# Two chunked scans: log decays by a mask matmul, or by cumulative sums broadcast from DRAM

## The reference

```
a_cs  = cumsum(adt)                       # over the 128 steps of a chunk
decay = exp(a_cs[l] - a_cs[s])  for s <= l, else 0
y_diag = (c . b) * decay @ (x * dt)
```

## Time and profile before

| | |
|---|---|
| time, three runs | median 1102.46 us (1102.23 to 1104.29) |
| profiled execution, first to last instruction | 1102.2 us |
| TensorE busy | 1065.5 us, 97% |
| VectorE busy | 662.8 us, 60% |
| ScalarE busy | 442.9 us, 40% |
| GpSimd busy | 215.7 us, 20% |
| DMA | 123.89 MB, 112 GB/s over the span |
| granted TensorE clock, mean | 0.988 |

### The profile page before, as it was taken

How to read it: one execution, slowest core, us unless ns; L and a number is a source line. 1 busy time by engine, 2 the same in 40 slices (tenths; PEclk the granted TensorE clock), 3 DMA queues, 4 the chain that set the end, 5 groups by cost and what they waited for, 6 DMA issues and landing times. The chain is left out here.

```text
span 1102.2 us, 14509 instructions
## 1 busy us (share of the span) xinstructions
PE 1065.5 (97%) x5590; PEld 876.1 (79%) x5590; DVE 662.8 (60%) x1139; ACT 442.9 (40%) x826; POOL 215.7 (20%) x161
## 2 busy tenths in 40 slices
PE   9999999999989999999899999999999988989997
PEld 5888888888778877788778788887888866878886
DVE  4246435741056687766736866666595667966635
ACT  4223224332256562231623334348624448225432
POOL 0000000000000052201300100002104754135792
PEclk9999999999989999999999999999999999999999
DMA  8276634322042050232324345435212231203501
GB/s 301 81 271 215 215 102 145 114 80 95 11 136 56 10 197 5 73 134 77 125 77 153 115 153 191 153 115 172 91 63 77 63 111 58 77 20 103 185 1 77
DMA packets 58306, 123.89 MB, mean 112 GB/s; under 512 B 5760, under 2 KB 6016, under 8 KB 58112
## 3 DMA queue, kind: packets, MB, share of 16 engines
q1 hardware_dynamic: 55792, 110.22, 29.9%
q0 software_dynamic: 2304, 12.58, 3.2%
q10 hardware_dynamic: 144, 0.20, 0.0%
HBM read 108.83 MB, written 14.16 MB: 112 GB/s over the span
## 5 line engine op out<-in xcount | busy, mean ns | idle before, releaser
L287 DVE TENSOR_TENSOR w_lo<-raw,w_hi 128x2048 fp32r<-128x2048 f32 x58 | 134.3, 2315 | 207.9 <-ACT w_hi L283 196.9
L283 ACT ACTIVATE w_hi<-raw 128x2048 fp32r<-128x2048 f32 x51 | 97.6, 1913 | 211.4 <-PE projections_ps L131 138.3
L129 PE MATMUL projections_ps<-projections_x_hi,w_hi 128*128 128x512 f32 x208 | 81.1, 390 | 0.4 <-ACTq L506 0.4
L130 PE MATMUL projections_ps<-projections_x_lo,w_hi 128*128 128x512 f32 x208 | 80.9, 389 | 0.0
L131 PE MATMUL projections_ps<-projections_x_hi,w_lo 128*128 128x512 f32 x208 | 80.9, 389 | 0.0
L129 PE MATMUL projections_ps<-w_hi,projections_x_hi 128*128 128x512 f32 x192 | 74.7, 389 | 0.0
L130 PE MATMUL projections_ps<-w_lo,projections_x_hi 128*128 128x512 f32 x192 | 74.7, 389 | 0.0
L131 PE MATMUL projections_ps<-w_hi,projections_x_lo 128*128 128x512 f32 x192 | 74.7, 389 | 0.0
L244 DVE SCALAR_TENSOR_TENSOR resid<-resid,mixer_cw 128x512 f32<-128x512 f32 x96 | 64.9, 745 | 0.0
L2480 POOL TENSOR_TENSOR mixer_es<-masks,mixer_gsel 128x1024 f32<-128x1024 f32 x8 | 17.3, 2165 | 229.5 <-PE mixer_ps L1902 152.2
L129 PE MATMUL output_ps<-w_hi,output_m_hi 128*128 128x512 f32 x128 | 52.9, 413 | 2.5 <-DVE output_m_lo L1267 1.4
(11 more groups left out here) (330 smaller groups left out, 2583.3 us busy)
## 6 DMA issues: line engine op xcount, KB each, us to landing
raw<-in_w_in SPq DMA_DIRECT2D x26, 1024.0 KB, 5.0
raw<-in_gdn_w_in SPq DMA_DIRECT2D x24, 1024.0 KB, 5.0
tok<-in_ada_w POOLq DMA_DIRECT2D x16, 768.0 KB, 6.3
raw<-in_w_out SPq DMA_DIRECT2D x8, 1024.0 KB, 5.0
qkv_kept<-mixer_ring SPq DMA_DIRECT2D x8, 1024.0 KB, 4.2
mixer_st<-qkv_kept SPq DMA_DIRECT2D x32, 256.0 KB, 2.9
raw<-in_gdn_w_out SPq DMA_DIRECT2D x8, 1024.0 KB, 5.1
resid<-in_att_bias SPq DMA_DIRECT2D x16, 256.0 KB, 2.7
```

Of the source, the lines that this page charges most:

```text
L129: nc.tensor.matmul(out, w_hi, x_hi, start=first, stop=False, skip_group_check=True)
L130: nc.tensor.matmul(out, w_hi, x_lo, start=False, stop=False, skip_group_check=True)
L283: self.nc.scalar.activation(self.hi[s][:], self.raw[s][:], ACT.Copy).then_inc(self.hi_ready, 1)
L287: engine.tensor_tensor(self.lo[s][:], self.raw[s][:], self.hi[s][:], ALU.subtract)\
```

## The change

The decay matrix is now exp(-relu(c_l - c_s)), s in the partitions,, from cumulative sums c = -cumsum(log decay).

1. Two small float32 matmuls with `upper` make all cumulative sums of a layer, once with rows of heads and chunks (`logs_t`) and once with the 128 steps in the partitions (`logs`); ScalarE copies both out, negated. In layer one this stands at the start of attention; in layer two ahead of convolution block 4 (`LOGS_AT`), and the last column tile of that block's first half waits until the bank is read.
2. SP writes `logs_t` to DRAM, and later loads one row of 1024 values for each step, broadcast to the 128 partitions (512 KB), into `steps_in` or `steps`. The place of each load in SP's list is in the diff.
3. GpSimd subtracts the column of the partition's own step in place, for all 8 matrices in one instruction.
4. ScalarE clips with Relu in place, then takes Exp with scale -1.
5. The `below` matmuls, their PSUM banks and the waits on `seg_made` go; so do `gsel` and its copy on VectorE. GpSimd starts its list in the second mixer with a wait for `logs_out` and clears a stage's semaphores there.

```diff
 # scan stage, SP
+            def load_logs(s):
+                g = s % G
+                if s >= G:
+                    sp.wait_ge(e_ok, s - 1)
+                sp.dma_start(steps_in[:, g].rearrange("p h l -> p (h l)"), a["logs"][s].partition_broadcast(P))\
+                    .then_inc(logs_in[g], 16)
+            sp.wait_ge(logs_kept, 16)
+            for s in range(G):
+                load_logs(s)
             sp.dma_start(resid[:], a["x"].rearrange("(t p) d -> p t d", p=P)).then_inc(rows_in, 16)
...
-            for u in range(2, 6):
+            for u in range(2, 4):
                 load_unit(u)
+            for s in range(G, STEPS - 1):
+                load_logs(s)
+            for u in range(4, 6):
+                load_unit(u)
+            load_logs(STEPS - 1)
 # scan stage, PE (ahead_of)
-                pe.wait_ge(steps_ok, s + 1)
-                if s:
-                    pe.wait_ge(e_ok, s)
-                for n in range(2):
-                    mm = nc.tensor.matmul(ps[:, SEG + n, :], below, steps_in[:, g, 4 * n:4 * n + 4, :]...)
-                mm.then_inc(seg_made, 1)
 # scan stage, ACT (ahead_of)
-                act.wait_ge(seg_made, s + 1)
+                act.wait_ge(steps_ok, s + 1)
                 if s >= G:
                     act.wait_ge(yd_made, s - 1)
-                nc.scalar.activation(E[:, g], ps_seg, ACT.Exp).then_inc(e_ok, 1)
+                nc.scalar.activation(steps_in[:, g], steps_in[:, g], ACT.Relu).then_inc(clipped, 1)
+                act.wait_ge(clipped, s + 1)
+                nc.scalar.activation(E[:, g], steps_in[:, g], ACT.Exp, scale=-1.0).then_inc(e_ok, 1)
 # scan stage, GpSimd
             def scan_steps(s):
-                if s >= G:
-                    pool.wait_ge(seg_made, s - 1)
-                nc.gpsimd.tensor_tensor(steps_in[:, g], upper..., adt[:, c, heads_of(g)]..., ALU.mult)
+                pool.wait_ge(logs_in[g], 16 * (s // G + 1))
+                here = logs[:, c, heads_of(g)].unsqueeze(2).broadcast_to([P, HPG, P])
+                nc.gpsimd.tensor_tensor(steps_in[:, g], steps_in[:, g], here, ALU.subtract).then_inc(steps_ok, 1)
 # second mixer, SP
+            def load_logs(i, j):
+                if j:
+                    sp.wait_ge(e_ok, at(i, 1, j - 1, 1))
+                elif i:
+                    sp.wait_ge(z_ok, 8 * (HB - 1))
+                else:
+                    sp.wait_ge(logs_kept, 16 * TT)
+                sp.dma_start(flat(steps), a["logs2"][i * HB + j].partition_broadcast(P)).then_inc(logs_in, 16)
...
             stage(0, 2)
+            load_logs(0, 1)
             load(B_CONV + 2)
             sp.wait_ge(kk_made, at(0, 1, 1, 1))
             stage(0, 3)
+            load_logs(0, 2)
             sp.wait_ge(kk_made, at(0, 1, 2, 1))
             stage(0, 0)
+            load_logs(0, 3)
             load(B_CONV + 3)
...
             stage(1, 0)
+            load_logs(1, 0)
...
             sp.wait_ge(kk_made, at(1, 1, 0, 1))
             stage(1, 2)
+            load_logs(1, 1)
             sp.wait_ge(kk_made, at(1, 1, 1, 1))
             stage(1, 3)
+            load_logs(1, 2)
             sp.wait_ge(kk_made, at(1, 1, 2, 1))
             stage(1, 0)
+            load_logs(1, 3)
 # second mixer, ACT
             def exps(i, j):
-                act.wait_ge(seg_made, at(i, 1, j, 1))
+                act.wait_ge(steps_ok, at(i, 1, j, 1))
...
-                nc.scalar.activation(E, psZ[:]..., ACT.Exp).then_inc(e_ok, 1)
+                nc.scalar.activation(steps, steps, ACT.Relu).then_inc(clipped, 1)
+                act.wait_ge(clipped, at(i, 1, j, 1))
+                nc.scalar.activation(E, steps, ACT.Exp, scale=-1.0).then_inc(e_ok, 1)
```

More of the change, by code:

```diff
@@ L298, in channels @@
             for e in range(4):
+                if s == 0 and e == 3 and before_last:
+                    before_last()
                 for kk in range(HALF):
@@ L665, in _, with attention @@
                     w.tokens(pe, i * 2 + (N_Z + j), (N_Z + j) % 2, ps, x_hi, x_lo, banks_free)
-def attention(nc, a, ahead, mix_in, raw, m_g, resid, masks, qk, vals, tok, bias_in):
+def attention(nc, a, ahead, mix_in, raw, m_g, resid, masks, qk, vals, tok, bias_in, adt, logs, logs_t, logs_kept):
     ctx = Phase(nc, "attention")
@@ L767, in values @@
                     pe.wait_ge(y_done, 4 * (h - 1))
+                if n == 0 and h == 1:
+                    pe.wait_ge(logs_out, 2)
                 for qt in PARTS[n]:
@@ L776, in _ @@
             scores(0)
+            nc.tensor.matmul(ps_o[0:LOGS, 1, 0:P], flat_adt, masks[:, UPPER, :], start=True, stop=True)
+            nc.tensor.matmul(ps_o[:, 1, P:P + LOGS], masks[:, UPPER, :], flat_adt, start=True, stop=True).then_inc(logs_made, 1)
             for h in range(ATT_HEADS):
@@ L868, in _, with scan_and_output @@
                     exponentials(a_next, TILES[3:])
-def scan_and_output(nc, a, ahead, wba, wba_in, mix_in, split, raw, att_f, m_g, masks, small, resid, row_f, tok, xbc, dt, adt, modc,
-                    g_col, gain):
+def scan_and_output(nc, a, ahead, wba, wba_in, mix_in, split, raw, att_f, m_g, masks, small, resid, row_f, tok, xbc, dt, adt, logs,
+                    logs_kept, modc, g_col, gain):
     w_v = a["w_out"][0].rearrange("(k p) c -> p k c", p=P)
@@ L925, in scan_and_output @@
         turned, m_hi_ok, m_lo_ok = sem("turned"), sem("m_hi_ok"), sem("m_lo_ok")
-        steps_ok, seg_made, e_ok = sem("steps_ok"), sem("seg_made"), sem("e_ok")
+        steps_ok, clipped, e_ok = sem("steps_ok"), sem("clipped"), sem("e_ok")
+        logs_in = [sem(f"logs_in{i}") for i in range(G)]
         xs_turned, xs_out, x_read, xskip_ok = sem("xs_turned"), sem("xs_out"), sem("x_read"), sem("xskip_ok")
@@ L1433, in second_mixer @@
     NB, HB = 2, 4
+    ended = Phase.take_used()
     ctx = Phase(nc, "mixer2")
@@ L1688, in _ @@
                 if n == 6:
+                    sp.wait_ge(logs_out, 2)
+                    rows_out = a["logs2"].rearrange("r (x c l) -> c (r x) l", c=TT, l=P)
+                    for c in range(TT):
+                        sp.dma_start(rows_out[c], logs_t[V_HEADS * c:V_HEADS * (c + 1), :]).then_inc(logs_kept, 16)
                     sp.wait_ge(spilled[0], 32)
@@ L1692, in _ @@
                         stage(0, j)
+                    load_logs(0, 0)
             load(B_CONV + 1)
@@ L1821, in _, with logs_read @@
             tr.then_inc(ba_made, 1)
+            def logs_read():
+                pe.wait_ge(logs_out, 2)
             for n in range(1, B_CONV):
-                w.channels(pe, n, n % 2, ps, h_hi, h_lo, banks_free)
+                if n == LOGS_AT:
+                    pe.wait_ge(banks_free, n + 1)
+                    pe.wait_ge(g_ok, 1)
+                    bank = ps[:, 4 * (n % 2) + 3, :]
+                    nc.tensor.matmul(bank[0:LOGS, 0:P], flat(g[:]), upper, start=True, stop=True)
+                    nc.tensor.matmul(bank[:, P:P + LOGS], upper, flat(g[:]), start=True, stop=True).then_inc(logs_made, 1)
+                w.channels(pe, n, n % 2, ps, h_hi, h_lo, banks_free, logs_read if n == LOGS_AT else None)
             pe.wait_ge(banks_free, B_CONV + 1)
@@ L1895, in build @@
                 mm.then_inc(kk_made, 1)
-                pe.wait_ge(steps_ok, at(i, 1, j, 1))
-                if j:
-                    pe.wait_ge(e_ok, at(i, 1, j - 1, 1))
-                if i and j == HB - 1:
-                    pe.wait_ge(m_lo_ok, 8)
-                for n in range(2):
-                    mm = nc.tensor.matmul(psZ[:, n, :], below, flat(steps[:, 4 * n:4 * n + 4, :]), start=True, stop=True)
-                mm.then_inc(seg_made, 1)
             def turn_v(i, j):
@@ L1912, in turn_v @@
                 else:
-                    pe.wait_ge(e_ok, at(1, 1, HB - 1, 1))
+                    pe.wait_ge(m_lo_ok, 8)
                     pe.wait_ge(yp_out, 6)
@@ L2102, in _ @@
                     build(1, 2)
-                    pe.wait_ge(e_ok, at(1, 1, 2, 1))
                     turn_m(6, 4)
@@ L2532, in begin @@
                 nc.gpsimd.memset(Uf.rearrange("p (a b) -> p a b", b=33)[:, :, 0], 1.0).then_inc(eye_ok, 1)
+            pool.wait_ge(logs_out, 2)
+            clear_semaphores(pool, ended)
             begin(0)
```

61 lines of the change are left out of this document (36 added, 25 removed).

## The result

The changed kernel takes 1116.88 us (median of 4 runs, 1115.36 to 1119.75), the kernel before in the same session 1102.35 us (4 runs): ratio 1.0137, 95% interval 1.0119 to 1.0156, 14.5 us or 1.4% slower. The forecast was 1109.5: the direction and the range held, the size was half of what came.

A forecast was written before the change was run, and what follows sets the result against it. TensorE was taken as full in the scan and first block, not the second; removed matmuls could save at most 27.4 us, but waits decide. 0.45 + 2.4 + 0.45 + 1.4 + 2.7 = +7.4 on 1102.2: 1109.5 us, range 1100 to 1117.

The forecast's parts named there:

- the scan is lost to the factor: Scan: late rows hold up GpSimd's factor, delaying group 1 by 5.3 us, +7.0 with the clock; whole stage +2.4.
- rival A: Scan: the factor is not held up, stage -6.7 instead of +2.4, total 1100.5 us; chance 0.14.
- The first block is lost to ScalarE's order: First block: Relu, exponential and table load delay a copy; TensorE waits 5.8 us before z unit 6; +1.4 us in all.
- The second block's pace: Second block: load, subtraction, clip and exponential on one tile put exponentials 7.9 us apart; +2.7 us.
- Rival D: Row loads in scan and both blocks: the broadcast itself is slow, 9.3 us; +28 us, 1137; chance 0.05.
- rival E: ScalarE, second mixer: Relu brings table loads of 1.28 us each, twice a step; up to +15 us, 1125; chance 0.02.
- No table load may stand beside a Relu: Sign for the changed trace: ScalarE shows no table load, 1.28 us each, next to any Relu.
- Ahead of convolution block 4 TensorE is full ... 4 records are 0.45 us: Second layer's log sums: their added matmuls on a full TensorE cost 0.45 us (0.3 to 0.8).
- the weight rest: Scan, steps 4 and 5: these pairs save nothing and VectorE's `rest(3)` stands 0.2 to 0.9 us later; +0.5.
- Steps 6 and 7: End of the scan: removed matmuls save 1.7 us in each of these steps, 3.4 in the stage's sum.
- Attention: Attention stage: the two new matmuls are free, ScalarE's additional copies cost 0.45 us (at most 0.5, low end nothing).
- the row of step 3 must be in the tile by some 402: Scan: the condition for rival A, by which factor and add keep their time and the stage is -6.7 us.

The follow-up runs named there:

- e4: Changed kernel with e1's filler; in the scan GpSimd makes the factor ahead of step 2's subtraction, loads unmoved: 1103.58 us, ratio 1.0015.
- e9: e7 with ScalarE's copies of z units 4 and 5 ahead of pair 2's clip and exponential in the first block: 1097.97 us, ratio 0.9952.
- e7: e4 with a second tile for the second mixer's log rows, used by odd pairs: 1103.56 us, ratio 1.0004.
- e1: Changed kernel with the unused filler tile 16 numbers wide, not 48, so the activation halves start at a multiple of 256 bytes: 1112.79 us, ratio 1.0086.
- e2: Kernel before with only the filler tile widened from 48 to 80 numbers, halves starting 128 bytes past a multiple of 256: 1108.92 us, ratio 1.0054.
- e6: Kernel before's attention and scan with the changed second mixer and e1's filler: 1108.30 us, ratio 1.0051.
- e8: Kernel before with the changed kernel's attention stage only, its result unread: 1100.90 us, ratio 0.9988.
- e3: Changed kernel with e1's filler; SyncE loads the log rows of scan steps 2 and 3 ahead of weight unit 3: 1110.46 us, ratio 1.0066.
- e5: Changed attention and scan with e4's factor-first order, second mixer of the kernel before: 1098.07 us, ratio 0.9950.
- e14: e9 with the load of pair 1's row moved behind the gate projection's first two weight halves: 1096.58 us, ratio 0.9938.

## Why the prediction was right in direction and half in size

**Held.** The range held by 0.1 us, with a cost in the measured time that no term of the forecast had; that is luck. What held by its mechanism: the scan is lost to the factor: `add_group(0)` forecast 7.1 us later, 8.35 later relative to the stage; the pause before group 1 is there and ended by that add; e4, which takes the factor alone out from behind the rows, gives back 8 us, where the distance between the forecast and rival A was 9.1. The first block is lost to ScalarE's order: the pause forecast at 5.8 us before z unit 6 is 4.79 and ended by that copy, and e9 shows it; with the row early (e7) 3.35 us of pause are left, where the forecast had 4.7. The second block's pace was forecast at 7.9 us a turn and is 7.6 to 7.9, with a load of 3.7 (3.6), a subtraction of 1.92 (1.9), clip and exponential of 1.06 each (1.03). Rival D (slow broadcast) is excluded by the same rows, rival E by the count of table loads, 15 in both traces. The sign "No table load may stand beside a Relu" was put too strictly: four stand between the clip and the exponential, and they are the exponential's. The Trainium skill's figure for the load (DMA: Bandwidth & Descriptors, "Anatomy of one DMA"), an estimate of 3.2 us, was 0.5 short of the 3.7 in the trace; the section fits it to transfers that GpSimd issues, and these are SyncE's.

**The step that failed: "Ahead of convolution block 4 TensorE is full ... 4 records are 0.45 us".** The price of the stage was taken from the instructions the diff adds to it. What the diff does to the stage's other matmuls was no term at all: it moves the tiles they read by 640 bytes. That is 5 to 6 of the 7.4 us by which the forecast was short (e1, e2). In the traces 3.1 (the changed kernel against e1) and 3.5 (e2) lie in the convolution stage, 1.0 and 2.2 in the first block; the second block's stage is not lengthened by it. It could have been asked from the diff: tiles are allocated in order, and an unused tile of 48 numbers stood right ahead of the halves. The log sums themselves cost 1.1 us (e1, e6), not 0.45.

**Terms that were mis-sized.** The scan +4.9, not +2.4. SyncE issued unit 3 1.2 us later in the stage than forecast (`rest(1)` was to end earlier and ended later), and row, factor and add came as much later: the add by 8.35 us and not 7.1, group 1 by 7.0 and not 5.3. With the clock behind the pause the late factor had cost 8.15 by the second add, not 7.0; the next iterations gave back 1.9 (forecast 1.7), and the weight rest then cost another 1.4 (forecast 0.5), since TensorE paused 3.35 us for `rest(3)` at 449.34 and ran at a clock of 0.76 behind it. Steps 6 and 7 gave back 2.8, not 3.4. The first block +2.4 with the address taken out, not +1.4. The second block +2.2, not +2.7. Attention -1.3 (e8), not +0.45: I priced ScalarE's copies, and what decided was the clock. The base was off too: the profiled 1102.2 us is a span, and belongs to an execution of 1104.29; on the median the sum gives 1109.9 and not 1109.5.

**Rival A** fixed its point of decision wrongly: "the row of step 3 must be in the tile by some 402" was not reached by the one order of SyncE that was tried (e3), and it isn't needed. The factor can be taken from behind the rows in GpSimd's order (e4), and then the scan gains, but less than A said: the stage is 1.8 to 4.4 us shorter in the seven traces with that order (2.2 in e4, 3.7 in e5), A had 6.7.

**Open.** Why the clock falls in attention in some executions and not in others behind the same work; which part of a start address decides the matmul's pace, since 32, 64 and 128 bytes were tried and no multiple of 256 but those of the kernel before and e1.

## What to carry to other kernels

A change of tiles is a change of addresses: when a diff adds or removes a buffer ahead of the operands of dense matmuls, compare the mean ns of an untouched matmul before and after, and pin the operands' start before judging the idea. A new wait on an engine with an ordered list is priced by what stands behind it in that list, and is often cheaper to dodge there (one factor moved ahead: 8 us; one copy moved ahead: 5.7 us) than to shorten. Taking work from a full engine gives time only where the next engine in line has slack: of 27.4 us of matmuls removed here, the best version (e14) keeps 6.8.

## What was not expected of the hardware

A 128x512 matmul whose operand tile starts at a multiple of 256 bytes of a partition (two such starts were run) takes 389 ns by its record; at 32 or 128 bytes past one it takes 395, and at 64 bytes past 388 to 394, as much when the tile is the streamed operand (convolution stage) as when it is the one loaded as weights (z products between 795 and 835 us: 389 in the kernel before and e1, 395 in the changed one and e2). The Trainium skill (SBUF — State Buffer, "Operand start alignment") asks only for a start at a multiple of the element size, which all these starts have, and says that its runs timed nothing; the 5 to 6 us of e1 and e2 are beside that rule, not against it.
